# Four mixer groups streamed with a two-part moving operand, and a convolution's chain one slot sooner

## The chip, the core and the metric

The kernel runs on one core of a Trainium2 chip, in one launch. The metric is the time of an execution on the device in microseconds (us); the median of three runs stands below. The core's engines are TensorE (PE in the profile; its weight loads are PEld), VectorE (DVE), ScalarE (ACT), GpSimd (POOL) and SyncE (SP). Each runs its own list of instructions in order and waits on semaphores for the others.

## The reference, cut to what matters

256 positions of width 2048 go through one layer of a first block (four attention branches, gates, an output projection) and one layer of a second. The change lies in the second block's mixers, between the first block's output projection and the second's:

```
z = rms(h, norm_mix_g) @ w_in_2            # 2048 -> 4096 columns
za, zb, zc, zd = split(z, (1024, 2560, 3584))
# za: u, v = gelu(za);  oa = u * (tril(w_s) @ layernorm(v) + b_s)
# zb: h, bg, cg;        ob = bg * conv3(cg * h)
# zc: a, g;  h = conv31(a * sigmoid(g)) + b;  oc = silu(layernorm(h))
# zd: od = (windowed means of zd - zd) @ pool_w * pool_scale
h = h + concat(oa, ob, oc, od) @ w_out_2
```

Before it stand the attention branches, behind it a gated feed-forward of width 5632 and a last gated projection. Everything is float32 and nearly all of the time is matmuls.

## The kernel before, in words

**Units.** Each float32 matmul is made of three in the fp32r type: a weight W is split into a high part `hi` (a rounded copy by ACT, L855) and a low part `lo` = W - hi (DVE, L1244), the activations likewise into XH and XL (or YH and YL, MH and ML), and PE adds hi·XH, hi·XL and lo·XH. The weights come in 370 **units** of 128 x 2048 elements (1 MB), which `plan` (L66) lists in order. SP loads unit u into `raw[u % 5]` once unit u-5 is done, ACT makes `hi[u % 4]`, DVE makes `lo` (which takes raw's place), PE uses both. ACT and DVE work three units ahead (AHEAD): in step u each does its extra work of that step (`side(u)`), then splits unit u+3, then takes the finished group's result out of PSUM (`post`). PE does `side(u)`, then `unit(u)`.

**Kinds.** A group is a block of columns of a weight, in one of three kinds. "N" has the activations as the stationary operand. "T" has the weights stationary, and the result comes out transposed: 16 tiles of 128 x 128 in a unit, and for each three matmuls that stream 256 columns (`three`, L476 to L479), 48 in all. "T2", so far used for queries and keys alone, also has the weights stationary, but streams XH and XL as one operand of 512 columns (L530), so that hi·XH and hi·XL land beside each other in PSUM, and then, behind a wait for `lo`, lo·XH with 256 columns (L534): 16 and 16 matmuls in a unit. The two sums of a T2 group are added afterwards: ACT copies one out (L1091), DVE adds the other (L1653), one group being half as wide as a T group.

**PSUM.** Group results alternate between the two halves of `psA`; a group may start once the group two before it has been read (`bank_act`, `bank_dve`).

**The stretch of the change.** The groups after the first block's projection are cf 0 and 1 (units 170 to 177: the conformer's a and g, half each), v2 (178 to 181, kind N), u2 (182 to 185), zd (186 to 189), scc (190 to 193), sch (194 to 197), bg (198 to 201), then out2 (202 to 217). Beside them DVE works off the 31-tap convolution (`conv_tap`, L1443 and L1445): 124 instructions on 128 x 256, seven in a step from step 177 on, the last four in step 194. Their end lets PE sum over the channels (`channel_sum`, L749) in step 196. From there a chain goes back and forth: mean (ACT, L1045), centring (DVE, L1581), squares (ACT, L1047), second channel sum (PE, step 198), reciprocal root and scaling (DVE, step 198), affine and tanh (ACT, 199), product and parts (200). The pool mixer's sums stand in steps 194 and 195, its matmuls (L799) in 198. The parts of oa, ob, oc and od go to YH and YL, and out2 takes them in the order of MIX_ORDER.

Of the kernel before, what the change touches and what calls it, by code (L numbers as in the profile page):

```python
# [18 lines left out]
H = 4  # L19
# [43 lines left out]
MIX_ORDER = (0, 3, 2, 1)  # L63


def plan(A):  # L66
# [60 lines left out]
def build_hybrid(nc, A, C, out, scratch):  # L127
    with ExitStack() as ctx:
# [101 lines left out]
        SQ = PW[:, 0:2, :].rearrange("p g d -> p (g d)")  # L230
# [97 lines left out]
        def halves(g):  # L328

            name, n = g.name  # L330
            dst, n = (QI, n + 1) if name == "qi" else ({"q": QT, "k": KT}[name], n % 2)
            return dst[:, 2 * n:2 * n + 2, :]
# [10 lines left out]
        EARLY = (196, 199, 200)  # L343
# [131 lines left out]
        def tensor_program(e):  # L475
# [14 lines left out]
            def await_operand(g, i):  # L490
                name, n = g.name
                if name == "narrow" or g.kind == "T2":
                    e.wait_ge(xl_made, 2 * i + 2)
                elif name in ("qi", "z", "v", "q", "k", "gate"):
                    e.wait_ge(xl_made, i + 1)
                elif name == "branch":
                    e.wait_ge(flip_low, n % 4 + 1)
                elif name == "out":
                    e.wait_ge(flip_low, MERGED + i + 1)
                elif name in ("cf", "v2", "u2", "zd", "scc", "sch", "bg"):  # L500
                    e.wait_ge(flip_low, FIRST + i + 1)
                elif name == "out2":
                    e.wait_ge(mix_low, i + 1)
                elif name in ("fg", "fu"):
                    e.wait_ge(flip_low, SECOND + i + 1)
                elif name == "down":
                    e.wait_ge(flip_low, HIDDEN + 4 * (n // 4) + i + 1)
                elif name == "proj":
                    e.wait_ge(pt_made, 1)
                else:  # L510
                    e.wait_ge(flip_low, THIRD + i + 1)

            def unit(u):
# [12 lines left out]
                if g.kind == "T2":  # L526
# [6 lines left out]
                    for n, (c, kb, s, both) in enumerate(places):  # L533
                        x = e.matmul(both[:, 256:512], ll[:, s], XH[:, kb, :], start=False,  # L534
                                     stop=i == len(g.parts) - 1 and n >= 14, skip_group_check=True)
                    x.then_inc(unit_done, 1)
# [215 lines left out]
            def side(u):  # L752
# [87 lines left out]
        def scalar_program(e):  # L840
# [112 lines left out]
            def side(u):  # L953
# [58 lines left out]
                if u in (176, 185):  # L1012
                    h = (176, 185).index(u)
                    cs = slice(2 * h, 2 * h + 2)
                    e.wait_ge(bank_dve, freed(("cf", h)))
# [19 lines left out]
                if u == 191:  # L1035
                    e.wait_ge(bank_dve, freed(("u2", 0)))
                    gelu_inner(B[:, 3, :], B[:, 2, :])
# [5 lines left out]
                if u == 196:  # L1043
# [4 lines left out]
                if u == 198:  # L1048
                    e.wait_ge(pool_dotted, 1)
                    for g in range(4):  # L1050
                        x = e.activation(YH[:, 12 + g, :], c4(psB[:, 1, :])[:, g, :], ACT.Copy, scale=VC[:, 76 + g:77 + g])
                    x.then_inc(mix_high, 1)
                if u == 199:
# [5 lines left out]
                if u == 200:  # L1059
                    e.wait_ge(cn_made, 1)  # L1060
                    part_high(CA[:, :, :], 2, 0.5)
                if u in TURN2:
# [12 lines left out]
            def post(g):  # L1075
# [10 lines left out]
                elif g.kind == "T2":  # L1086
# [3 lines left out]
                    e.wait_ge(unit_done, g.last + 1)  # L1090
                    e.activation(halves(g), sums(g)[1], ACT.Copy).then_inc(crossed, 1)  # L1091
                elif name == "qi":
# [37 lines left out]
                elif name == "bg":  # L1130
                    e.wait_ge(bank_dve, g.freed)
                    part_high(c4(B[:, 3, :]), 1, 1.0)
# [68 lines left out]
        def vector_program(e):  # L1201
# [262 lines left out]
            def pool_sums():  # L1464
                e.memset(P1[:, :, 0:16], 0.0)
                e.memset(P2[:, :, 0:16], 0.0)
                e.wait_ge(bank_dve, freed(("zd", 0)))
# [15 lines left out]
            def side(u):  # L1483
# [90 lines left out]
                if u == 194:  # L1574
                    part_low(c4(B[:, 3, :]), 0, 0.5, 1)
                    pool_sums()
                if u == 195:
                    pool_means()
                if u == 196:
                    e.wait_ge(cm_made, 1)  # L1580
                    e.tensor_tensor(CA[:, :, :], CA[:, :, :], over(ST[:, 0, :], 4), ALU.subtract).then_inc(ca_centered, 1)  # L1581
                if u == 198:
# [4 lines left out]
                    e.tensor_tensor(CA[:, :, :], CA[:, :, :], over(y_, 4), ALU.mult).then_inc(ca_normed, 1)  # L1587
                    y = c4(B[:, 2, :])
# [6 lines left out]
                if u == 199:  # L1595
                    y = c4(B[:, 2, :])
                    for j in (1, 2):
                        for c in range(4):
# [3 lines left out]
                                                   op0=ALU.mult, op1=ALU.add).then_inc(short_taps, 1)  # L1602
                    e.wait_ge(short_taps, 12)
                    finish(e.tensor_tensor(y, y, over(SB[:, :], 4), ALU.mult))
                if u == 200:
                    e.wait_ge(cn_tanh, 1)
                    e.scalar_tensor_tensor(out=CA[:, :, :], in0=CB[:, :, :], scalar=1.0, in1=CA[:, :, :], op0=ALU.add,
                                           op1=ALU.mult).then_inc(cn_made, 1)
                    e.wait_ge(mix_high, 2)
# [4 lines left out]
                    part_low(CA[:, :, :], 2, 0.5, 3)  # L1614
# [28 lines left out]
            def post(g):  # L1643
# [6 lines left out]
                elif g.kind == "T2":  # L1650
                    dst = halves(g)
                    e.wait_ge(crossed, g.crossed)
                    x = e.tensor_tensor(dst, sums(g)[0], dst, ALU.add)  # L1653
                    if name == "k":
                        finish(x)
                        e.wait_ge(rx_copied, 1)
                        x = e.tensor_tensor(dst, dst, over(RX[:, :], 2), ALU.mult)
                    x.then_inc(bank_dve, 1)
                elif name == "branch":
# [19 lines left out]
                elif name == "cf":  # L1679
                    cs = slice(2 * n, 2 * n + 2)  # L1680
                    e.wait_ge(unit_done, g.last + 1)
                    e.wait_ge(sb_made, 1)
                    e.tensor_tensor(CA[:, cs, :], c4(ps)[:, 0:2, :], over(SB[:, :], 2), ALU.mult)
                    e.tensor_tensor(CB[:, cs, :], c4(ps)[:, 2:4, :], over(SB[:, :], 2), ALU.mult).then_inc(bank_dve, 1)
                elif name == "u2":
                    e.wait_ge(unit_done, g.last + 1)
                    e.tensor_tensor(c4(B[:, 3, :]), c4(ps), over(SB[:, :], 4), ALU.mult).then_inc(bank_dve, 1)
                elif name == "zd":
                    e.memset(PA[:, :, 0:16], 0.0)
                    e.wait_ge(unit_done, g.last + 1)  # L1690
                    e.tensor_tensor(PA[:, :, 16:272], c4(ps), over(SB[:, :], 4), ALU.mult).then_inc(bank_dve, 1)
# [13 lines left out]
                elif name == "bg":  # L1705
                    t = c4(B[:, 3, :])
                    e.wait_ge(unit_done, g.last + 1)
                    e.tensor_tensor(t, c4(ps), c4(B[:, 2, :]), ALU.mult).then_inc(bank_dve, 1)
                    part_low(t, 1, 1.0, 4)
# [148 lines left out]
```

## Time and profile before

| what | us |
|---|---|
| median of 3 runs (lowest, highest) | 2116.52 (2116.45, 2117.03) |
| the profiled execution, its own time | 2116.6 |
| its span, first to last instruction | 2114.8 |
| PE busy in the span | 2101.7 (99%), 10607 matmul records |
| DVE busy | 1215.1 (57%) |
| ACT busy | 901.8 (43%) |
| granted TensorE clock, mean | 0.999 of full |

The profile is of one execution. A page gives the busy time of each engine and the chain of work that ended last. The views of the trace used below give single instructions in order of time (the timeline), the busy time by stretch (windows), and that chain in order of time. A matmul's record lasts longer than the distance to the next one, since they overlap: the pace is read from starts. A float32 matmul that isn't fp32r shows as two records.

### The profile page before, as it was taken

How to read it: one execution, taken by the hardware profiler on the slowest of the kernel's cores; microseconds unless marked ns; L12 is line 12 of the kernel's file. 1: busy time of each engine (PE TensorE's matmuls, PEld its weight loads, DVE VectorE, ACT ScalarE, POOL GpSimd, SP SyncE). 2: the span in 40 equal slices, each digit the busy share in tenths (PEclk: the TensorE clock that was granted, in tenths of full speed). 3: DMA queues.
4: the chain of work that ended last, by engine and by line, in shares of the span. 5: the costliest groups of instructions: out<-in, count | busy, mean ns of one | idle time of the engine just before them, and what ended most of it. 6: DMA issues, size and time to landing. Idle time of an engine off the chain costs nothing.

```text
span 2114.8 us, 24862 instructions
## 1 busy us (share of the span) xinstructions
PE 2101.7 (99%) x10607; PEld 1788.5 (85%) x10607; DVE 1215.1 (57%) x1211; ACT 901.8 (43%) x858; POOL 21.1 (1%) x40
## 2 busy tenths in 40 slices
PE   9999999999999999999999999999999999999998
PEld 8888888888888888888999888888888888888887
DVE  5576555665545544456889855545445454454555
ACT  5444443544443443445354444343333433334443
POOL 2000000000000000000000000000000000000000
PEclk9999999999999999999999999999999999999999
DMA  8655555555655555575655556555555555565553
GB/s 245 212 178 178 166 171 182 171 175 173 199 182 196 192 188 197 192 246 180 206 187 171 179 179 195 189 187 191 198 188 191 184 194 196 187 195 182 195 201 120
DMA packets 224685, 398.34 MB, mean 188 GB/s; under 512 B 11154, under 2 KB 56458, under 8 KB 224320
## 3 DMA queue, kind: packets, MB, share of 16 engines
q1 hardware_dynamic: 221296, 387.64, 56.0%
q0 software_dynamic: 2528, 8.00, 1.3%
q8 instruction: 84, 1.38, 0.3%
q10 hardware_dynamic: 752, 1.12, 0.1%
q14 instruction: 25, 0.20, 0.0%
HBM read 394.62 MB, written 2.12 MB: 188 GB/s over the span
## 4 chain that ended last, share of the span: by engine, by line
PE 95%; DVE 4%; ACT 1%; issue 0%; ACTq 0%
PE psA L477 27%; PE psA L479 27%; PE psA L478 27%; PE psA L530 6%; PE psA L534 3%; DVE CA L1445 1%; PE psB L589 1%; DVE lo L1244 1%; PE psB L689 0%; PE psB L715 0%; PE psA L826 0%; PE psB L637 0%; PE psB L749 0%; ACT hi L855 0%; PE psB L676 0%
## 5 line engine op out<-in xcount | busy, mean ns | idle before, releaser
L1244 DVE TENSOR_TENSOR lo<-raw,hi 128x2048 fp32r<-128x2048 f32 x369 | 837.1, 2272 | 618.2 <-ACT hi L855 616.0
L855 ACT ACTIVATE hi<-raw 128x2048 fp32r<-128x2048 f32 x369 | 699.6, 1900 | 685.4 <-PE psA L479 583.2
L477 PE MATMUL psA<-hi,XHL 128*128 128x512 f32 x1632 | 637.9, 391 | 0.0
L479 PE MATMUL psA<-hi,XHL 128*128 128x512 f32 x1632 | 633.9, 388 | 0.0
L478 PE MATMUL psA<-lo,XHL 128*128 128x512 f32 x1632 | 633.4, 388 | 0.0
L479 PEld LDWEIGHTS psA<-hi,XHL 128*128 128x128 f32 x1632 | 306.3, 188 | 63.6
L477 PEld LDWEIGHTS psA<-hi,XHL 128*128 128x128 f32 x1632 | 306.5, 188 | 62.6 <-issue 0.4
L478 PEld LDWEIGHTS psA<-lo,XHL 128*128 128x128 f32 x1632 | 306.6, 188 | 61.7
L477 PE MATMUL psA<-hi,YH 128*128 128x512 f32 x608 | 237.2, 390 | 0.0
L479 PE MATMUL psA<-hi,YL 128*128 128x512 f32 x608 | 236.6, 389 | 0.0
L478 PE MATMUL psA<-lo,YH 128*128 128x512 f32 x608 | 236.6, 389 | 0.0
L477 PE MATMUL psA<-XHL,hi 128*128 128x256 f32 (+1 forms) x528 | 150.2, 284 | 1.2 <-DVE lo L1284 1.2
L478 PE MATMUL psA<-XHL,hi 128*128 128x256 f32 (+1 forms) x528 | 149.3, 283 | 0.0
L479 PE MATMUL psA<-XHL,lo 128*128 128x256 f32 (+1 forms) x528 | 149.3, 283 | 0.0
L530 PE MATMUL psA<-XHL,hi 128*128 128x512 f32 x576 | 138.6, 393 | 0.0
L479 PEld LDWEIGHTS psA<-hi,YL 128*128 128x128 f32 x608 | 114.1, 188 | 23.7
L477 PEld LDWEIGHTS psA<-hi,YH 128*128 128x128 f32 x608 | 114.1, 188 | 23.5
L478 PEld LDWEIGHTS psA<-lo,YH 128*128 128x128 f32 x608 | 114.2, 188 | 23.4
L530 PEld LDWEIGHTS psA<-XHL,hi 128*128 128x128 f32 x576 | 105.9, 188 | 21.5 <-issue 0.6
L477 PEld LDWEIGHTS psA<-XHL,hi 128*128 128x128 f32 (+1 forms) x528 | 100.7, 191 | 1.7 <-DVE XHL L1291 1.6
L478 PEld LDWEIGHTS psA<-XHL,hi 128*128 128x128 f32 (+1 forms) x528 | 100.7, 191 | 0.2
L479 PEld LDWEIGHTS psA<-XHL,lo 128*128 128x128 f32 (+1 forms) x528 | 100.7, 191 | 0.0
(355 smaller groups left out, 1273.6 us busy)
## 6 DMA issues: line engine op xcount, KB each, us to landing
raw<-in_w_in_dram SPq DMA_DIRECT2D x159, 1024.0 KB, 5.1
raw<-in_w_gate_dram SPq DMA_DIRECT2D x44, 1024.0 KB, 5.2
raw<-in_w_up_dram SPq DMA_DIRECT2D x44, 1024.0 KB, 5.2
raw<-in_w_down_dram SPq DMA_DIRECT2D x44, 1024.0 KB, 5.1
raw<-in_w_out_dram SPq DMA_DIRECT2D x32, 1024.0 KB, 5.1
raw<-in_w_branch_dram SPq DMA_DIRECT2D x16, 1024.0 KB, 5.0
raw<-in_w_ple_gate_dram SPq DMA_DIRECT2D x16, 1024.0 KB, 5.0
raw<-in_w_in_dram SPq DMA_DIRECT2D x16, 512.0 KB, 4.7
```

The lines of the kernel that those rows point to most:

```text
L477: e.matmul(dst, A2[0], B2[0], start=first, stop=False, skip_group_check=True)
L478: e.matmul(dst, A2[0], B2[1], start=False, stop=False, skip_group_check=True)
L479: return e.matmul(dst, A2[1], B2[0], start=False, stop=last, skip_group_check=True)
L530: e.matmul(both, hh[:, s], XHL[:, kb, :, :].rearrange("p a t -> p (a t)"), start=i == 0 and n < 2, stop=False, skip_group_check=True)
L534: x = e.matmul(both[:, 256:512], ll[:, s], XH[:, kb, :], start=False, stop=i == len(g.parts) - 1 and n >= 14, skip_group_check=True)
L589: x = e.transpose(ps[:, k, 128 * t:128 * t + 128], src(t, k), ID[:, :])
L855: e.activation(hi[u % H][:, 0:m], raw[u % R][:, 0:m], ACT.Copy).then_inc(hi_made, 1)
L1244: e.tensor_tensor(lo[u % R][:, 0:m], raw[u % R][:, 0:m], hi[u % H][:, 0:m].bitcast(F32), ALU.subtract).then_inc(lo_made, 1)
L1445: x = e.scalar_tensor_tensor(out=CA[:, c, :], in0=HP[:, c, j:j + 256], scalar=CW[:, 4 * j + c:4 * j + c + 1], in1=CA[:, c, :], op0=ALU.mul ...
```

## The change

- In `plan`, cf 1 becomes two T2 groups (cf 1: the a half, cf 2: the g half, both of the second 256 columns), and u2, zd and bg become two T2 groups each. They cover the same units as before (174 to 177, 182 to 189, 198 to 201); a unit is now 8 blocks of rows by 256 columns instead of 4 by 512. The count of groups grows by four.
- The T groups that stay (cf 0, scc, sch) do all hi·XH and hi·XL of a unit first, then wait for `lo`, then do the 16 lo·XH.
- The first channel sum of PE moves from step 196 to 195, the second from 198 to 197, and the steps of ACT and DVE that hang on them with them (centring before the pool's means; scaling in 197; affine and tanh in 198; product in 199). The 124 taps stay in the steps where they were.
- The pool's first sums move from step 194 to 195 and its means from 195 to 196; its matmuls stay in 198. out2 takes the blocks in the order 0, 2, 3, 1.
- `post` of the new T2 groups: an ACT copy, a DVE addition and a DVE product (with SB, or for bg with the short convolution) for each half.

```diff
-MIX_ORDER = (0, 3, 2, 1)
+MIX_ORDER = (0, 2, 3, 1)
@@ plan
-    for h in range(2):
-        group(("cf", h), "T", w_in2, (2560 + 256 * h, 3072 + 256 * h), K16)
+    group(("cf", 0), "T", w_in2, (2560, 3072), K16)
+    for n in (1, 2):
+        group(("cf", n), "T2", w_in2, 2304 + 512 * n, K8)
...
-        group((name, 0), "T", w_in2, col, K16)
+        if name in ("scc", "sch"):
+            group((name, 0), "T", w_in2, col, K16)
+        else:
+            for h in range(2):
+                group((name, h), "T2", w_in2, col + 256 * h, K8)
@@ tensor_program, unit
-                if g.kind == "T2":
+                if g.kind == "T2" or g.kind == "T" and u >= H:
                     e.wait_ge(hi_made, u + 1)
...
+                if g.kind == "T" and u >= H:
...
+                    for j, c, kb, s, dst in places:
+                        e.matmul(dst, hh[:, s], XH[:, kb, :], start=i == 0 and j == 0 and c % 2 == 0, stop=False,
+                                 skip_group_check=True)
+                        e.matmul(dst, hh[:, s], XL[:, kb, :], start=False, stop=False, skip_group_check=True)
+                    e.wait_ge(lo_made, u + 1)
+                    for j, c, kb, s, dst in places:
+                        x = e.matmul(dst, ll[:, s], XH[:, kb, :], start=False, stop=i == len(g.parts) - 1 and j == 3,
+                                     skip_group_check=True)
...
@@ tensor_program, side
-                if u == 196:
+                if u == 195:
                     e.wait_ge(conv_taps, 124)
                     e.wait_ge(sw_made, 1)
                     channel_sum(psB[:, 0, 0:256], CA, cm_dotted)
...
-                if u == 198:
+                if u == 197:
                     e.wait_ge(cv_squared, 1)
                     channel_sum(psB[:, 0, 512:768], CB, var_dotted)
@@ vector_program, side
                 if u == 194:
                     part_low(c4(B[:, 3, :]), 0, 0.5, 1)
+                if u == 195:
                     pool_sums()
-                if u == 195:
-                    pool_means()
-                if u == 196:
                     e.wait_ge(cm_made, 1)
                     e.tensor_tensor(CA[:, :, :], CA[:, :, :], over(ST[:, 0, :], 4), ALU.subtract).then_inc(ca_centered, 1)
-                if u == 198:
+                if u == 196:
+                    pool_means()
+                if u == 197:
@@ vector_program, post
                 elif g.kind == "T2":
                     dst = halves(g)
+                    if name == "zd" and n == 0:
+                        e.memset(PA[:, :, 0:16], 0.0)
                     e.wait_ge(crossed, g.crossed)
                     x = e.tensor_tensor(dst, sums(g)[0], dst, ALU.add)
...
+                    elif name in ("cf", "u2", "zd"):
+                        finish(x)
+                        e.wait_ge(sb_made, 1)
+                        x = e.tensor_tensor(dst, dst, over(SB[:, :], 2), ALU.mult)
                     x.then_inc(bank_dve, 1)
...
-                    e.tensor_tensor(c4(B[:, 3, :]), c4(ps), over(SB[:, :], 4), ALU.mult).then_inc(bank_dve, 1)
```

The order on PE around the first channel sum, before. L477, L478 and L479 are hi·XH, lo·XH and hi·XL (the operands' printed order is moving, then stationary), L744 the sgu mixer's eight matmuls behind unit 193, L749 the channel sum; between L744 and L749 stand units 194 and 195, 96 matmuls:

```order
L744 MATMUL psB<-SW,B 128x128 x8
L477 MATMUL psA<-XHL,hi 128x256
L478 MATMUL psA<-XHL,hi 128x256
...
L479 MATMUL psA<-XHL,lo 128x256
L749 MATMUL psB<-CA,TR 128x256 x4
L477 MATMUL psA<-XHL,hi 128x256
```

And after (L554 and L556 are hi·XH and hi·XL, L559 lo·XH, L769 the mixer's matmuls, L774 the channel sum):

```order
L769 MATMUL psB<-SW,B 128x128 x8
L554 MATMUL psA<-XHL,hi 128x256
L556 MATMUL psA<-XHL,hi 128x256
...
L559 MATMUL psA<-XHL,lo 128x256 x16
L774 MATMUL psB<-CA,TR 128x256 x4
L554 MATMUL psA<-XHL,hi 128x256
```

The channel sum now has one unit (194) between it and the mixer's matmuls, where it had two.

The order on DVE from u2's result to zd's, before (L1687 reads u2 out of PSUM, L1691 zd; SM rows of a small reciprocal root left out):

```order
L1687 TENSOR_TENSOR B<-psA,SB 128x1024
L1443 TENSOR_SCALAR CA<-HP,CW,VC 128x256 x2
L1445 SCALAR_TENSOR_TENSOR CA<-HP,CW,CA 128x256 x7
...
L1244 TENSOR_TENSOR lo<-raw,hi 128x2048
L1689 MEMSET B 128x4x16
L1691 TENSOR_TENSOR B<-psA,SB 128x4x256
```

After (L1682 adds a half's two sums, L1693 multiplies by SB, L1270 makes `lo`, L1469 and L1471 are the taps). First u2's second half, then zd's first and second:

```order
L1682 TENSOR_TENSOR B<-psA,B 128x512
L1693 TENSOR_TENSOR B<-B,SB 128x512
L1469 TENSOR_SCALAR CA<-HP,CW,VC 128x256 x2
L1471 SCALAR_TENSOR_TENSOR CA<-HP,CW,CA 128x256 x7
...
L1682 TENSOR_TENSOR B<-psA,B 128x2x256
L1693 TENSOR_TENSOR B<-B,SB 128x2x256
...
L1270 TENSOR_TENSOR lo<-raw,hi 128x2048
L1682 TENSOR_TENSOR B<-psA,B 128x2x256
L1693 TENSOR_TENSOR B<-B,SB 128x2x256
```

One instruction of 128 x 1024 has become four of 128 x 512, two for each half, and the first half's pair stands two splits ahead of the second's; u2's first pair stands in step 183.

## Rows read from the trace of the kernel before

**Rows 1.** The page: busy time; the chain that ended last, by engine.

```profile
PE 2101.7 (99%) x10607; PEld 1788.5 (85%) x10607; DVE 1215.1 (57%) x1211; ACT 901.8 (43%) x858; POOL 21.1 (1%) x40
...
PE 95%; DVE 4%; ACT 1%; issue 0%; ACTq 0%
```

**Rows 2.** Windows: length; busy PE, PEld, DVE, ACT, POOL; the second, DVE alone.

```profile
1107.00:1153.00 46.00, 45.75 (x376) 45.34 (x376) 45.62 (x71) 18.55 (x13) 0.00 (x0) 1.00 0.52 163
...
1087.10:1143.60 56.50, 55.95 (x96) 1.00 0.55 179
```

**Rows 3.** PE's timeline: first matmuls of units 190, 191, 195; channel sum.

```profile
1106.95 0.28 PE L477 MATMUL psA<-XHL,hi 128*128 128x256 f32 x1
...
1112.71 0.28 PE L477 MATMUL psA<-XHL,hi 128*128 128x256 f32 x1
...
1137.53 0.28 PE L477 MATMUL psA<-XHL,hi 128*128 128x256 f32 x1
...
1143.70 1.99 PE L749 MATMUL psB<-CA,TR 128*128 128x256 f32 x8 [0.25 <-DVE CA L1445]
```

**Rows 4.** PE's timeline: T2 units 51 and 52, hi part.

```profile
318.48 3.82 PE L530 MATMUL psA<-XHL,hi 128*128 128x512 f32 x16
...
324.04 3.82 PE L530 MATMUL psA<-XHL,hi 128*128 128x512 f32 x16
```

**Rows 5.** DVE's timeline, 1065 to 1144: waits, posts, taps.

```profile
1065.27 2.29 DVE L1244 TENSOR_TENSOR lo<-raw,hi 128x2048 fp32r<-128x2048 f32 x1 [2.02 <-ACT hi L855]
...
1087.07 2.29 DVE L1244 TENSOR_TENSOR lo<-raw,hi 128x2048 fp32r<-128x2048 f32 x1 [3.52 <-ACT hi L855]
1089.28 1.22 DVE L1687 TENSOR_TENSOR B<-psA,SB 128x1024 f32<-128x1024 f32 x1
1090.41 0.73 DVE L1443 TENSOR_SCALAR CA<-HP,CW,VC 128x256 f32<-128x256 f32 x2
...
1103.73 2.86 DVE L1445 SCALAR_TENSOR_TENSOR CA<-HP,CW,CA 128x256 f32<-128x256 f32 x7
...
1113.73 0.11 DVE L1689 MEMSET B<- 128x64 f32 x1
...
1114.83 2.86 DVE L1445 SCALAR_TENSOR_TENSOR CA<-HP,CW,CA 128x256 f32<-128x256 f32 x7
...
1141.98 1.67 DVE L1445 SCALAR_TENSOR_TENSOR CA<-HP,CW,CA 128x256 f32<-128x256 f32 x4
```

**Rows 6.** DVE's timeline: a key half's post; a product of 128 x 512.

```profile
347.20 0.69 DVE L1653 TENSOR_TENSOR KT<-psA,KT 128x512 f32<-128x512 f32 x1 [1.96 <-ACT KT L1091]
347.93 0.69 DVE L1657 TENSOR_TENSOR KT<-KT,RX 128x512 f32<-128x512 f32 x1
...
1039.90 0.68 DVE L1684 TENSOR_TENSOR CB<-psA,SB 128x512 f32<-128x512 f32 x1
1040.50 2.85 DVE L1445 SCALAR_TENSOR_TENSOR CA<-HP,CW,CA 128x256 f32<-128x256 f32 x7
```

**Rows 7.** ACT's timeline, ahead of DVE's two waits.

```profile
1061.08 0.69 ACT L1125 ACTIVATE B<-psA,SM 128x512 f32<-128x512 f32 x1 [3.23 <-PE psA L479]
...
1063.34 1.90 ACT L855 ACTIVATE hi<-raw 128x2048 fp32r<-128x2048 f32 x1
...
1083.58 0.40 ACT L1026 ACTIVATE B<-B,SM 128x128 f32<-128x128 f32 x1 [8.47 <-DVE SM L1560]
```

**Rows 8.** Windows at the end; the granted clock is third from last.

```profile
2105.00:2106.00 1.00, 0.20 (x2) 0.00 (x0) 0.20 (x1) 0.77 (x3) 0.00 (x0) 1.00 1.02 379
...
2109.00:2110.00 1.00, 0.00 (x0) 0.00 (x0) 0.93 (x3) 0.64 (x2) 0.00 (x0) 0.73 0.00 0
2110.00:2112.00 2.00, 0.00 (x0) 0.00 (x0) 0.51 (x2) 0.70 (x2) 0.00 (x0) 0.50 0.52 194
```

**Rows 9.** PE's timeline at the start: the same float32 matmul first and later.

```profile
2.02 4.64 PE L826 MATMUL psA<-QI 128*128 128x256 f32 x10 [2.02 <-DVE QI L1751]
...
8.61 1.89 PE L831 MATMUL psB<-QI 128*128 128x256 f32 x8
```

More of the change, by code:

```diff
@@ L330, in halves @@
             name, n = g.name
-            dst, n = (QI, n + 1) if name == "qi" else ({"q": QT, "k": KT}[name], n % 2)
+            if name == "cf":
+                return (CA, CB)[n - 1][:, 2:4, :]
+            if name == "zd":
+                return PA[:, 2 * n:2 * n + 2, 16:272]
+            n = n + 1 if name == "qi" else n % 2
+            dst = {"qi": QI, "q": QT, "k": KT}[name] if name in ("qi", "q", "k") else c4(B[:, 3, :])
             return dst[:, 2 * n:2 * n + 2, :]
@@ L491, in await_operand @@
                 name, n = g.name
-                if name == "narrow" or g.kind == "T2":
+                if name in ("narrow", "qi", "q", "k") and len(g.parts) == 2:
                     e.wait_ge(xl_made, 2 * i + 2)
+                elif g.kind == "T2":
+                    e.wait_ge(flip_low, FIRST + 2 * i + 2)
                 elif name in ("qi", "z", "v", "q", "k", "gate"):
@@ L535, in unit @@
                                      stop=i == len(g.parts) - 1 and n >= 14, skip_group_check=True)
+                    x.then_inc(unit_done, 1)
+                    return
+                if g.kind == "T" and u >= H:
+                    places = [(j, c, kb, slice(512 * j + 128 * c, 512 * j + 128 * c + 128), ps[:, 256 * c:256 * c + 256])
+                              for j, (_, kb) in enumerate(part) for c in range(4)]
+                    for j, c, kb, s, dst in places:
[6 more added lines that the diff above has]
+                                     skip_group_check=True)
                     x.then_inc(unit_done, 1)
@@ L1048, in side @@
                 if u == 198:
[L1049 to L1053, printed above, removed]
                     e.wait_ge(ca_normed, 1)
@@ L1058, in side @@
                     e.activation(CB[:, :, :], CA[:, :, :], ACT.Tanh, scale=0.5).then_inc(cn_tanh, 1)
-                if u == 200:
+                if u == 199:
                     e.wait_ge(cn_made, 1)
                     part_high(CA[:, :, :], 2, 0.5)
+                    e.wait_ge(pool_dotted, 1)
+                    for g in range(4):
+                        x = e.activation(YH[:, 12 + g, :], c4(psB[:, 1, :])[:, g, :], ACT.Copy, scale=VC[:, 76 + g:77 + g])
+                    x.then_inc(mix_high, 1)
                 if u in TURN2:
@@ L1090, in post @@
                     e.wait_ge(unit_done, g.last + 1)
+                    if name == "bg":
+                        e.wait_ge(pool_dotted, 1)
                     e.activation(halves(g), sums(g)[1], ACT.Copy).then_inc(crossed, 1)
+                    if name == "bg" and n == 1:
+                        e.wait_ge(bank_dve, g.freed)
+                        part_high(c4(B[:, 3, :]), 1, 1.0)
                 elif name == "qi":
@@ L1587, in side @@
                     e.tensor_tensor(CA[:, :, :], CA[:, :, :], over(y_, 4), ALU.mult).then_inc(ca_normed, 1)
+                if u == 198:
                     y = c4(B[:, 2, :])
@@ L1595, in side @@
                 if u == 199:
+                    e.wait_ge(cn_tanh, 1)
+                    e.scalar_tensor_tensor(out=CA[:, :, :], in0=CB[:, :, :], scalar=1.0, in1=CA[:, :, :], op0=ALU.add,
+                                           op1=ALU.mult).then_inc(cn_made, 1)
                     y = c4(B[:, 2, :])
@@ L1605, in side @@
                 if u == 200:
[L1606 to L1609, printed above, removed]
+                    e.wait_ge(mix_high, 3)
                     for g in range(4):
@@ L1679, in post @@
                 elif name == "cf":
-                    cs = slice(2 * n, 2 * n + 2)
                     e.wait_ge(unit_done, g.last + 1)
                     e.wait_ge(sb_made, 1)
[L1683 to L1686, printed above, removed]
-                    e.tensor_tensor(c4(B[:, 3, :]), c4(ps), over(SB[:, :], 4), ALU.mult).then_inc(bank_dve, 1)
[L1688 to L1691, printed above, removed]
+                    e.tensor_tensor(CA[:, 0:2, :], c4(ps)[:, 0:2, :], over(SB[:, :], 2), ALU.mult)
+                    e.tensor_tensor(CB[:, 0:2, :], c4(ps)[:, 2:4, :], over(SB[:, :], 2), ALU.mult).then_inc(bank_dve, 1)
                 elif name == "scc":
```

27 lines of the change are left out of this document (12 added, 15 removed).

## The prediction

> **What bounds the kernel now.** First the page: PE is busy for 2101.7 of 2114.8 us and the chain that ended last lies on PE for 95% [rows 1]. So in general only PE's pace counts. Then the windows of the stretch that is changed: from 1107 to 1153 us PE is busy 45.75 of 46.00 us, but DVE 45.62 of 46.00 [rows 2]. Here two engines are full at once, and the 4% of the chain on DVE come from such places. Then PE's timeline around the channel sum: it starts at 1143.70 after 0.25 us of idleness that a DVE write of CA ended, the last tap of the convolution [rows 3], which ended at 1141.98 + 1.67 = 1143.65 [rows 5]. So in the kernel before the taps are just in time for step 196, with nothing to spare. DVE itself has no gap from 1087.07 to there: 55.95 busy of 56.50 us [rows 2], the rest being the short pauses between dependent instructions.
>
> **What T2 gives PE.** A T unit takes 1112.71 - 1106.95 = 5.76 us from start to start [rows 3], a T2 unit 324.04 - 318.48 = 5.56 [rows 4]. Sixteen units change kind (4 of cf, 4 of u2, 4 of zd, 4 of bg): 16 x 0.20 = 3.2 us, all on PE's path where PE is never short of operands. These rows say that per tile 512 columns at once cost 12 ns less than twice 256.
>
> The Trainium skill, page TensorE: Matmul & The Clock Gate, section Back-to-back issue gap, gives an isolated matmul N / 2.4 ns + 2.5 ns, by which a merged pair would save only 2.5 ns in a tile, about 0.04 us in a unit and 0.6 us in all where the rows give 3.2; the rows disagree with it, and the sum goes by the rows.
>
> **What `lo` last gives.** In the 12 T units that stay, the wait for `lo` comes two thirds of a unit later. No wait for `lo` shows on PE in the stretch before; same matmuls, same pace: nothing. Four groups more mean no more units or matmuls. The loads have other shapes, but each is issued five units, some 28 us, ahead, and of that `hi` and `lo` take 1.90 and 2.29 [rows 5, 7]: nothing. The order of out2's blocks follows the order in which they get ready: nothing.
>
> **What it costs DVE.** A product of 128 x 1024 out of PSUM takes 1.13 us of DVE for u2 (1089.28 to 1090.41) and 1.10 with its memset for zd (1113.73 to 1114.83) [rows 5]. A T2 half takes an addition (0.73 from its start to that of the next, dependent instruction) and a product (0.60, from 1039.90 to 1040.50) [rows 6], 1.33 in all. Four halves are 5.3 instead of 2.2: 3.1 us more before the last tap. Bounds: the product is 0.60 back to back and 0.73 with a pause, so 3.1 to 3.6. cf's halves (2.7 for 1.2) lie mostly in DVE's gaps before 1065, covered by its wait of 2.02 us there [rows 5]; bg's come after the taps.
>
> What gives DVE time back: that wait of 2.02 us at 1065.27 was ended by ACT's `hi` of 1063.34, which stood behind ACT's copies of v2 from 1061.08, released by PE [rows 5, 7]. PE gets there 4 units x 0.20 = 0.8 us sooner. The second wait (3.52 us, at 1087.07) was DVE's own doing: ACT's squares waited 8.47 us for a DVE result of gelu's chain, and `hi` stood behind them [rows 5, 7]; this round moves with DVE and stays as long. So the last tap moves by 3.1 - 0.8 = +2.3 us, to 1145.95.
>
> **What moving the channel sum costs PE.** This is the term that decides. The sum is now wanted one unit sooner, but the taps keep their steps and end 2.3 us later. From the start of the sum on PE has left what it had, and unit 195 too (5.76), less 4 bg units x 0.20 = 0.8. The end therefore moves by 2.3 + 5.76 - 0.8 = +7.3 us. Seen from PE: unit 194 ended at 1137.53 [rows 3]; with 12 T2 units before it, 2.4 us sooner, 1135.1. One small wait comes in between: unit 190 needs the half of PSUM that zd's first half used, and DVE reads it late: the taps at 1103.73 are preceded by it, so 1103.73 - 0.8 + 2 x 1.33 (u2's halves) - 1.13 + 0.05 + 0.73 + 0.69 = 1105.9, where PE arrives at 1106.95 - 2.4 = 1104.5: 1.4 us [rows 3, 5, 6]. PE then stands before the sum at 1136.5 and waits until 1145.95: 9.5 us, in place of 0.25. The wait at 190 isn't added, since it shortens the wait at 195.
>
> Queued behind the waiting sum is everything on PE: units 195 and on. ACT and DVE go on splitting ahead and fill their slots, so nothing else is late when PE starts again; the later steps of the chain keep their two-unit distance (195 to 197, where before 196 to 198) with the same matmuls. Step 198's pool matmuls get their operands in step 196, with two units to spare. I count these at 0; at worst one of them waits up to 3 us.
>
> **The clock.** PE's last matmul ends at 2105.2; the granted clock is still full until 2109 and at 0.50, that is 1.2 instead of 2.4 GHz, from within 2109 to 2110 on [rows 8]. A wait of 9.5 us is over twice that, so PE will find itself at half clock when the taps are done. No wait in the middle of the kernel before is long enough to show the way back. The start shows it: the first ten records of a 256-column float32 matmul took 4.64 us, eight of the same later 1.89, so ten would have been 2.3 [rows 9]: 2.3 us lost before the pace is full. I add 2.3, with 0 (the clock holds) and about 3.5 (the low level lasts half as long again) as ends.
>
> The Trainium skill says the same thing as a warning, in TensorE: Matmul & The Clock Gate, section Why this matters for your kernels: idle gaps between bursts of matmuls drop the array back to the lower clock. By this rule the sum is 9.6 us, without it 7.3; the trace agrees with it at the end of the kernel.
>
> **The sum.** Against the profiled execution: its span 2114.8 + 7.3 + 2.3 = 2124.4, and 1.8 around the span as before: 2126.2. Its time of 2116.6 is the median within 0.1, so the forecast is 2126.1 us, 9.6 (0.45%) more than 2116.52.
>
> **The rivals.**
> 1. The clock holds, or recovers at once: 2116.5 + 7.3 = 2123.8. For it: the mechanism is seen only at the ends of the kernel. Against it: the fall came 4 us into idleness there, and 9.5 are due here. 12%.
> 2. Not slower: DVE gets through in time and the sum doesn't wait. Then only 3.2 + 0.25 remain: 2116.5 - 3.4 = 2113.1, which is within 0.2%. This decides at the last tap: it would have to end by 1136.5 instead of 1145.95. Speaking for it would be slack in DVE's list, and the windows show 0.5 us of pauses in 56 [rows 2]; each tap depends on the one before the last on the same columns. 4%. That the change doesn't do what it says belongs here with its other sign: were the two-part operand no faster than two matmuls, as the skill's formula has it, DVE would get 0.2 back instead of 0.8 and bg save 0.2 instead of 0.8, which gives 2126.1 + 1.2 = 2127.3. 2%.
> 3. A second wait opens behind the first (centring behind the pool's sums, the second channel sum, or the pool's matmuls), up to 3 us: 2129. For it: DVE is still full until 1153 [rows 2]. Against it: PE's stop of 9.5 us lets DVE and ACT get ahead. 8%.
>
> **How the numbers follow.** Forecast 2126.1: 71%, own range 2124.8 to 2127.8 from the bounds of the clock and of the halves. Rivals 12, 4, 2, 8; the rest, 3%, is spread. The range 2122.5 to 2128.5 holds the forecast, the first rival and the skill's formula. A measurement of this kernel can tell about 0.2%, 4.2 us, from no change; the first rival and the third lie beyond it on the same side. Slower 0.93, same 0.06, faster 0.01.
>
> **What would show it.** Before the first channel sum PE idles 9 to 10 us, ended by a tap; before unit 190 1.4 us, ended by DVE's product of zd's first half; the granted clock falls to 0.50 in that wait and PE's matmuls run at half pace for some 4.6 us behind it; T2 units start 5.56 us apart; DVE is without gaps from 1088 to the last tap. I am wrong if the last tap ends before 1140, or if the wait before the sum is under 5 us; wrong in one term if the matmuls behind it keep their full pace.

## The result, and the profile after

| | median us (lowest, highest) |
|---|---|
| before, run beside it | 2116.48 (2116.40, 2117.03) |
| after | 2125.89 (2125.58, 2126.18) |
| ratio | 1.0043, 95% interval 1.0031 to 1.0056 |

The changed kernel is 9.4 us (0.43%) slower, and the interval of the ratio lies clear of 1. The profiled execution took 2125.58 us, with a span of 2123.8. Beside the experiments below the kernel before had medians of 2116.61 to 2116.75.

The page first: busy time of each engine, and the engines of the chain that ended last.

```profile
PE 2100.5 (99%) x10351; PEld 1776.7 (84%) x10351; DVE 1221.1 (57%) x1222; ACT 906.6 (43%) x866; POOL 21.2 (1%) x40
...
PE 95%; DVE 4%; ACT 1%; issue 0%; ACTq 0%
```

Against [rows 1] PE has 256 records fewer (16 units in which 32 matmuls became 16) and is busy 1.2 us less, while the span grew by 9.0. The shares are the same as before. A page on which PE is busy for 99% does not show where 9 us went; the waits of PE from 1040 to 1215 us do (line waited at, who ended it, total, times, longest):

```profile
PE psB L774 <- DVE CA L1471: 9.1, 1, 9.1
PE psA L554 <- DVE B L1693: 1.3, 1, 1.3
```

Two waits, and nothing else. In PE's timeline around them, first two T2 units of zd, then the first unit behind the short wait (190) and the next, then the end of unit 194, the channel sum behind the long wait, and the first matmuls of unit 195 behind it:

```profile
1093.31 3.82 PE L542 MATMUL psA<-XHL,hi 128*128 128x512 f32 x16
...
1098.88 1.32 PE L542 MATMUL psA<-XHL,hi 128*128 128x512 f32 x5
...
1105.90 0.35 PE L554 MATMUL psA<-XHL,hi 128*128 128x256 f32 x1 [1.30 <-DVE B L1693]
...
1111.73 0.28 PE L554 MATMUL psA<-XHL,hi 128*128 128x256 f32 x1
...
1134.63 2.08 PE L559 MATMUL psA<-XHL,lo 128*128 128x256 f32 x16
...
1145.82 3.78 PE L774 MATMUL psB<-CA,TR 128*128 128x256 f32 x8 [9.11 <-DVE CA L1471]
...
1149.04 0.74 PE L554 MATMUL psA<-XHL,hi 128*128 128x256 f32 x1
1149.61 0.28 PE L556 MATMUL psA<-XHL,hi 128*128 128x256 f32 x1
```

The T2 units start 5.57 us apart. The sum starts at 1145.82, where in the kernel before it started at 1143.70 with a whole unit more in front of it [rows 3]. From its start to the next unit's it takes 3.22 us, before 1.65 (1143.70 to 1145.35).

Windows of the same stretch (length; busy PE, PEld, DVE, ACT, POOL; granted clock; DMA share, GB/s):

```profile
1107.00:1153.00 46.00, 36.89 (x287) 35.97 (x287) 45.59 (x66) 17.90 (x15) 0.00 (x0) 0.89 0.42 132
...
1138.00:1139.00 1.00, 0.00 (x0) 0.00 (x0) 1.00 (x2) 0.00 (x0) 0.00 (x0) 1.00 0.79 152
1139.00:1140.00 1.00, 0.00 (x0) 0.00 (x0) 1.00 (x1) 0.00 (x0) 0.00 (x0) 0.68 0.92 310
...
1140.00:1145.00 5.00, 0.00 (x0) 0.00 (x0) 4.93 (x8) 0.79 (x1) 0.00 (x0) 0.50 0.31 110
1145.00:1149.00 4.00, 3.18 (x8) 2.56 (x9) 3.80 (x4) 3.87 (x3) 0.00 (x0) 0.50 0.00 0
1149.00:1150.00 1.00, 1.00 (x7) 0.91 (x6) 1.00 (x4) 0.36 (x1) 0.00 (x0) 0.70 0.00 0
1150.00:1151.00 1.00, 1.00 (x11) 1.00 (x10) 0.97 (x2) 0.02 (x1) 0.00 (x0) 1.00 0.00 0
```

Against [rows 2] PE is busy 36.89 of 46 us in place of 45.75, DVE as full as before. The granted clock falls to 0.50 (1.2 GHz) within 1139 to 1140, while PE stands, and is back at 1.00 (2.4 GHz) within 1149 to 1150, after some 3.8 us of matmuls. By the shares of these two windows it fell at about 1139.4, 2.7 us after PE's last record ended (1134.63 + 2.08 = 1136.71).

And DVE's timeline: the first wait of [rows 5], u2's two halves (1072.66, 1089.68), zd's two (1104.40, 1115.62), and the last taps.

```profile
1064.34 2.29 DVE L1270 TENSOR_TENSOR lo<-raw,hi 128x2048 fp32r<-128x2048 f32 x1 [1.26 <-ACT hi L880]
...
1072.66 0.68 DVE L1682 TENSOR_TENSOR B<-psA,B 128x512 f32<-128x512 f32 x1
1073.37 0.69 DVE L1693 TENSOR_TENSOR B<-B,SB 128x512 f32<-128x512 f32 x1
...
1087.47 2.29 DVE L1270 TENSOR_TENSOR lo<-raw,hi 128x2048 fp32r<-128x2048 f32 x1 [3.52 <-ACT hi L880]
1089.68 0.68 DVE L1682 TENSOR_TENSOR B<-psA,B 128x512 f32<-128x512 f32 x1
1090.40 0.69 DVE L1693 TENSOR_TENSOR B<-B,SB 128x512 f32<-128x512 f32 x1
...
1104.40 0.63 DVE L1682 TENSOR_TENSOR B<-psA,B 128x512 f32<-128x512 f32 x1
1105.07 0.69 DVE L1693 TENSOR_TENSOR B<-B,SB 128x512 f32<-128x512 f32 x1
...
1115.62 0.69 DVE L1682 TENSOR_TENSOR B<-psA,B 128x512 f32<-128x512 f32 x1
1116.35 0.69 DVE L1693 TENSOR_TENSOR B<-B,SB 128x512 f32<-128x512 f32 x1
...
1144.10 1.67 DVE L1471 SCALAR_TENSOR_TENSOR CA<-HP,CW,CA 128x256 f32<-128x256 f32 x4
```

The second wait of 3.52 us is as long as before [rows 5] and 0.40 later. The last tap ends at 1144.10 + 1.67 = 1145.77, 2.12 later than before, and DVE has no gap from 1087.47 to there.

### The profile page after: what moved, and what is told of

It reads as the page before. It is cut to its first block, busy times and chain, and to the rows that moved or that the text cites. A ratio compares the mean times of both kernels' runs of the same rounds, so it can differ in the third digit from the quotient of the medians.

```text
span 2123.8 us, 24372 instructions
## 1 busy us (share of the span) xinstructions
PE 2100.5 (99%) x10351; PEld 1776.7 (84%) x10351; DVE 1221.1 (57%) x1222; ACT 906.6 (43%) x866; POOL 21.2 (1%) x40
## 3 DMA queue, kind: packets, MB, share of 16 engines
HBM read 394.62 MB, written 2.12 MB: 187 GB/s over the span
## 4 chain that ended last, share of the span: by engine, by line
PE 95%; DVE 4%; ACT 1%; issue 0%; ACTq 0%
PE psA L487 26%; PE psA L489 26%; PE psA L488 26%; PE psA L542 8%; PE psA L546 4%; DVE CA L1471 1%; PE psB L614 1%; DVE lo L1270 1%; PE psA L554 1%; PE psA L559 1%; PE psA L556 1%; PE psB L774 0%; PE psB L714 0%; PE psB L740 0%; PE psA L851 0%
## 5 line engine op out<-in xcount | busy, mean ns | idle before, releaser
L1270 DVE TENSOR_TENSOR lo<-raw,hi 128x2048 fp32r<-128x2048 f32 x369 | 837.2, 2272 | 618.2 <-ACT hi L880 616.0
L542 PE MATMUL psA<-XHL,hi 128*128 128x512 f32 x832 | 200.0, 392 | 0.0
L542 PEld LDWEIGHTS psA<-XHL,hi 128*128 128x128 f32 x832 | 153.1, 188 | 30.8 <-issue 0.6
L546 PEld LDWEIGHTS psA<-XHL,lo 128*128 128x128 f32 x832 | 106.7, 191 | 4.1
L546 PE MATMUL psA<-XHL,lo 128*128 128x256 f32 x832 | 107.9, 283 | 0.0
L487 PE MATMUL psA<-hi,MH 128*128 128x512 f32 x128 | 50.2, 392 | 0.0
L489 PE MATMUL psA<-hi,ML 128*128 128x512 f32 x128 | 49.9, 390 | 0.0
L488 PE MATMUL psA<-lo,MH 128*128 128x512 f32 x128 | 49.8, 389 | 0.0
L1471 DVE SCALAR_TENSOR_TENSOR CA<-HP,CW,CA 128x256 f32<-128x256 f32 x120 | 49.0, 479 | 0.0
```

The costliest lines, as they stand in the source:

```text
L487: e.matmul(dst, A2[0], B2[0], start=first, stop=False, skip_group_check=True)
L488: e.matmul(dst, A2[0], B2[1], start=False, stop=False, skip_group_check=True)
L489: return e.matmul(dst, A2[1], B2[0], start=False, stop=last, skip_group_check=True)
L542: e.matmul(both, hh[:, s], XHL[:, kb, :, :].rearrange("p a t -> p (a t)"), start=i == 0 and n < 2, stop=False, skip_group_check=True)
L1270: e.tensor_tensor(lo[u % R][:, 0:m], raw[u % R][:, 0:m], hi[u % H][:, 0:m].bitcast(F32), ALU.subtract).then_inc(lo_made, 1)
L1471: x = e.scalar_tensor_tensor(out=CA[:, c, :], in0=HP[:, c, j:j + 256], scalar=CW[:, 4 * j + c:4 * j + c + 1], in1=CA[:, c, :], op0=ALU.mul ...
```

## The experiments

**The theory:** the 9.4 us are the sum wanted a unit sooner (5.76), the taps 2.3 us later, the clock that falls in the wait (about 2), less what bg gains (0.8). **The rivals:** the clock costs nothing; DVE's additional halves alone bring the loss; `lo` last costs or gives something; the merged operand gives nothing.

### The change with the chain in its old steps

```diff
-                if u == 195:
+                if u == 196:
                     e.wait_ge(conv_taps, 124)
...
-                if u == 197:
+                if u == 198:
                     e.wait_ge(cv_squared, 1)
```

and the steps of ACT and DVE that hang on them, the pool's steps and MIX_ORDER as before the change. The rest is the changed kernel.

> The changed kernel with the convolution's chain put back into the steps it had before (sums in steps 196 and 198, and what hangs on them); the T2 groups and lo last stay. Last-tap theory: the taps still end near 1145.7 on DVE (2.1 us later than before), PE reaches the sum one unit later, near 1142.4, and waits some 3.4 us; the end is 2.1 - 0.8 (four bg units at 0.2) = 1.3 us behind the kernel before: 2117.8 us; the wait is shorter than the 4 us after which the clock fell at the kernel's end, so the clock should hold. Rival, the T2 groups themselves are slow (their reading out of PSUM, their loads): the time stays near 2125.9.

Measured: 2119.84 us (2118.69 to 2120.82), ratio 1.0014 (1.0005 to 1.0023). The profiled execution is the 2118.69 one. PE's timeline at the sum:

```profile
1146.53 1.99 PE L774 MATMUL psB<-CA,TR 128*128 128x256 f32 x8 [3.35 <-DVE CA L1472]
```

And windows around it, columns as above:

```profile
1143.00:1146.00 3.00, 0.17 (x2) 0.00 (x0) 2.96 (x7) 1.08 (x2) 0.00 (x0) 1.00 0.49 115
1146.00:1148.00 2.00, 1.47 (x7) 1.32 (x8) 2.00 (x6) 2.00 (x2) 0.00 (x0) 1.00 0.98 339
```

In this execution the clock holds through the wait of 3.35 us. It starts 0.7 us late, in its first matmuls (16 transposes take 2.51 us where they took 1.97 in the kernel after); without that it stands at 2118.0, close to the 2117.8 that the terms gave. But the other nine executions are 1.0 to 2.1 us above the profiled one, with a mean clock of 0.998 or 0.997 instead of 0.999. I take it from this that the clock fell in them; none of the nine has a profile, so it is inferred and not shown. The chain's step is worth about 6 us (2125.89 - 2119.84), most of the loss. The median lies 2.0 us above what I expected, and by this reading the clock after a wait of 3.4 us is what I had wrong.

### The chain alone

The kernel before with the chain's edit alone (the diff above the other way round); all groups T.

> The kernel before with the convolution's chain one step sooner and nothing else. Last-tap theory: the taps end at 1143.65 as before, PE is there at 1137.5 and waits some 6 us; unit 195 comes behind the sum: + 5.8 us, and the clock, if 6 us of idleness are enough for it to fall, + 2.0: 2124.2 (2122.2 if it holds). Rival, the T2 groups are what is slow: 2116.5.

Measured: 2124.91 us (2123.95 to 2125.08), ratio 1.0037 (1.0024 to 1.0051). PE's timeline:

```profile
1143.70 3.57 PE L749 MATMUL psB<-CA,TR 128*128 128x256 f32 x8 [6.01 <-DVE CA L1444]
```

The taps end where they ended before [rows 5], the wait is a unit's 5.76 us + 0.25, and the sum takes 3.57 instead of 1.99: half clock. One edit alone makes 8.3 of the 9.4 us (2124.91 - 2116.61). In the profiled execution it is 7.3 us of span, the unit's 5.76 and 1.6 of half clock. The other four executions are 0.7 to 1.1 us slower than the profiled one, and no profile shows why; the expected 2124.2 was 0.7 short of the median.

### Matmuls in the wait, to keep the clock up

The changed kernel with 18 float32 matmuls of 256 columns ahead of the wait. They write where the sum writes afterwards, so their results are dropped.

```diff
                 if u == 195:
+                    e.wait_ge(sw_made, 1)
+                    for _ in range(18):
+                        e.matmul(psB[:, 0, 0:256], ONE, SB[:, :], start=True, stop=True)
                     e.wait_ge(conv_taps, 124)
```

> The changed kernel with 18 matmuls of 128x256 in float32 on PE ahead of the wait for the last tap, whose result the channel sum overwrites: about 7.8 us of work in a wait of 9.1. If the half clock behind the wait costs 2 us of its own, the clock now stays full, PE waits about 1.3 us, the sum's eight records take 2 us instead of 3.8, and the time is 2123.9. If the half clock is harmless, the time stays 2125.9; if the added matmuls don't fit into the wait, it is more.

Measured: 2124.24 us (2123.73 to 2124.52), ratio 1.0035 (1.0021 to 1.0048). PE's timeline:

```profile
1137.01 7.93 PE L817 MATMUL psB<-SB,TR 128*128 128x256 f32 x36
...
1146.30 1.99 PE L774 MATMUL psB<-CA,TR 128*128 128x256 f32 x8 [1.35 <-DVE CA L1474]
```

And two windows:

```profile
1136.00:1145.00 9.00, 8.95 (x46) 7.66 (x45) 8.93 (x14) 1.88 (x3) 0.00 (x0) 1.00 0.40 117
1145.00:1151.00 6.00, 4.70 (x33) 4.50 (x34) 5.80 (x9) 4.62 (x4) 0.00 (x0) 1.00 0.00 0
```

The taps end when they end, so the sum starts no sooner (it stands 0.5 us later than in the kernel after, since this execution was 0.5 us later from its first matmuls on). But it takes 1.99 us instead of 3.78, and the kernel is 1.65 us faster with 36 more matmul records. That difference of medians is what the half clock cost.

### Taps taken away

The changed kernel without 28 of the 124 taps, four in each of steps 187 to 193, so its result isn't the reference's.

```diff
-                    e.wait_ge(conv_taps, 124)
+                    e.wait_ge(conv_taps, 96)
...
-                    for j, c in some:
+                    for j, c in (some[:3] if 187 <= u <= 193 else some):
```

> The changed kernel without 28 of the 124 taps (four in each of steps 187 to 193), so the convolution's result is not the reference's; 28 x 0.395 = 11 us of DVE work less ahead of the last tap. Last-tap theory: the wait of 9.1 us is gone and with it the half clock, and what is left is the gain of 16 T2 units and the 0.25 us: 2113.0 to 2114 us, faster than the kernel before. Rival, something else in the moved chain or the new groups costs time: it stays above 2116.5.

Measured: 2113.22 us (2112.77 to 2113.64), ratio 0.9983 (0.9974 to 0.9993). PE waits nowhere from 1040 to 1215 us, and the sum follows unit 194 at once:

```profile
1133.12 2.08 PE L559 MATMUL psA<-XHL,lo 128*128 128x256 f32 x16
1135.05 1.89 PE L774 MATMUL psB<-CA,TR 128*128 128x256 f32 x8
```

Everything else of the change is in this kernel. So nothing of its loss lies in the loads, in `lo` last, in the order of the blocks or in a later step of the chain: it is that DVE ends the taps late.

### `lo` last alone

The kernel before; the 28 T units of its mixers do hi·XH and hi·XL first, then wait for `lo` (the branch of the change's diff). In the kernel before, L477, L478 and L479 are hi·XH, hi·XL and lo·XH, in this order: the third operand pair of each tile is what moves to the end. (The section on the change has L478 and L479 the wrong way round.)

> The kernel before with the other order inside its T units alone (hi parts first, then the wait for lo, then the 16 lo matmuls; 28 units of cf, u2, zd, scc, sch, bg), still 48 matmuls of 256 columns in a unit. My theory: no wait for lo showed on PE, same pace, 2116.5 as before within 0.3 us. Rival: the order brings something by itself (the same stationary tile twice in a row happens in both orders' hi part only now), then a T unit takes less than 5.76 us from start to start and the time falls by up to 3 us.

Measured: 2116.80 us (2116.27 to 2117.17), ratio 1.0000 (0.9990 to 1.0009). Beside it the kernel before had 2116.75. Nothing is gained and nothing lost that these runs can tell.

### T2 where DVE has time

The chain as before, `lo` last, T2 for cf 1 and bg alone; u2 and zd stay T with one product each, read out as before the change. The line in `plan`, against the first experiment's kernel:

```diff
-        if name in ("scc", "sch"):
+        if name in ("scc", "sch", "u2", "zd"):
```

> Two-part streaming for cf 1 and bg alone, u2 and zd as they were, the chain in the steps of before, lo last in the T units. Theory that the end is set by DVE up to the last tap: u2's and zd's halves are what made the taps later (3.1 us); without them the taps end 0.8 us sooner than before (1142.9), and bg's gain of 0.8 comes on top: 2116.5 - 1.6 = 2114.9, with a wait of 0.2 us before the sum. Rival, PE's pace sets it everywhere: 8 units less of T2 than in the first experiment make it slower than that one (2119.8), by 1.6 us: 2121.4.

Measured: 2115.15 us (2114.81 to 2115.68), ratio 0.9993 (0.9983 to 1.0002). PE waits for 0.27 us before the sum, as in the kernel before; the last taps start at 1141.11 instead of 1141.98. Eight units at 0.20 give 1.6 us (2116.75 - 2115.15), and they are kept, since their halves lie in DVE's gaps or behind the taps.

### Nine taps into DVE's own wait

To the change with the chain in its old steps comes a move on DVE: the second block's wait of 3.52 us is for ACT's squares, which stand behind DVE's means in step 185. The nine taps of step 186 (the first step of each half of the convolution has nine, the last four, those between seven) are put between, in step 185.

```diff
-                if u in CONV:
+                if u in CONV and u != 186:
...
                     e.tensor_scalar(gm, gm, -1.0 / 128, None, ALU.mult).then_inc(sgu_mean, 1)
+                    for j, c in CONV[186][1]:
+                        conv_tap(2 + c, j)
```

> The first experiment (all T2 groups, lo last, the chain in the steps of before), and the nine taps of step 186 put into step 185, into DVE's wait of 3.5 us for hi behind the mean of the sgu mixer. They take 3.4 us, so the last tap ends near 1142.3 to 1143 instead of 1146.5, and the wait of PE before unit 190 is gone too. Expected: PE waits some 1 to 2 us before the sum, too short for the clock to fall: 2114.5 to 2115. If DVE's wait was not idle time that taps can use (ACT's hi comes later then), the time stays at 2118.7 to 2119.8.

Measured: 2115.31 us (2114.74 to 2116.73), ratio 0.9995 (0.9986 to 1.0004). Six executions lie at 2114.74 to 2115.36, four at 2116.65 to 2116.73, so the median is one of a mixture; it lies above the expected 2114.5 to 2115. The profiled one is one of the four. PE's timeline at the sum:

```profile
1142.95 3.14 PE L774 MATMUL psB<-CA,TR 128*128 128x256 f32 x8 [1.78 <-DVE CA L1472]
```

And windows behind it:

```profile
1142.00:1143.00 1.00, 0.05 (x1) 0.05 (x1) 1.00 (x4) 1.00 (x2) 0.00 (x0) 1.00 0.62 122
1143.00:1144.00 1.00, 1.00 (x4) 0.88 (x5) 1.00 (x2) 1.00 (x1) 0.00 (x0) 0.82 0.89 230
...
1144.00:1147.00 3.00, 3.00 (x11) 2.55 (x11) 2.93 (x6) 3.00 (x3) 0.00 (x0) 0.50 0.68 232
1147.00:1148.00 1.00, 1.00 (x10) 1.00 (x10) 1.00 (x1) 1.00 (x2) 0.00 (x0) 0.97 0.00 0
```

Here the wait is 1.78 us, and the clock falls all the same, in 1143 to 1144, when PE is at work again. In this execution a wait of 1.78 us did not protect the clock. PE's wait before unit 190 is gone, as expected.

### And the first taps one step sooner

On top of that the first half's taps start in step 176 instead of 177, and each of its later steps takes the taps that follow:

```diff
-        CONV = {177 + 9 * h + i: (h, TAPS[2 + CHUNK * i if i else 0:2 + CHUNK * i + CHUNK]) for h in range(2) for i in range(9)}
+        SOON = ((9, 16, 23, 30, 37, 44, 51, 58, 62, 62), (0, 9, 16, 23, 30, 37, 44, 51, 58, 62))
+        CONV = {177 + 9 * h + i: (h, TAPS[SOON[h][i]:SOON[h][i + 1]]) for h in range(2) for i in range(9)}
...
                     conv_start(0)
+                    for j, c in TAPS[0:9]:
+                        conv_tap(c, j)
```

> The same, and the first nine taps of the convolution's first half moved from step 177 to 176, where DVE waited for hi before; every later step of that half does the taps of the step behind it, and step 185 none of them. No arithmetic is left out. 3.4 us less of DVE work in its full stretch; the last tap ends before PE gets to the sum in step 196, so PE should wait nowhere in the stretch and keep the whole gain of the 16 T2 units and the 0.25 us: 2113.0 to 2113.5, faster than both kernels. If another chain becomes the bound, a new wait shows on PE and the time lies above 2114.

Measured: 2112.89 us (2112.80 to 2113.43), ratio 0.9982 (0.9973 to 0.9992). This kernel is faster than both. The timeline, PE's sum and DVE's last taps:

```profile
1141.13 1.89 PE L775 MATMUL psB<-CA,TR 128*128 128x256 f32 x8
...
1138.74 1.67 DVE L1473 SCALAR_TENSOR_TENSOR CA<-HP,CW,CA 128x256 f32<-128x256 f32 x4
```

And the window that answers to [rows 2]:

```profile
1107.00:1153.00 46.00, 46.00 (x380) 45.79 (x380) 45.59 (x68) 15.85 (x13) 0.00 (x0) 1.00 0.56 176
```

The taps end at 1140.41, 0.7 us before they are wanted. PE is busy for the whole 46 us.

### Which part of that is the taps' own

The two moves of taps in the kernel before, all groups T:

> The kernel before with the two moves of taps of e10 alone (nine taps from step 176 on, nine in DVE's wait of step 185); all groups T, chain in its old steps. Theory: the kernel before loses 0.25 us at the channel sum and nothing else in this stretch, so taps that are done sooner can give back 0.25 us at most: 2116.2 to 2116.6. The gain of e10 is then the 3.2 us of the T2 units, which the taps only uncover. Rival: the order of the taps is worth something by itself (shorter waits of PE elsewhere); then this kernel is at 2114.5 or lower and e10 has only part of its gain from T2.

Measured: 2116.07 us (2115.86 to 2116.15), ratio 0.9997 (0.9987 to 1.0006). PE's timeline:

```profile
1143.22 1.89 PE L750 MATMUL psB<-CA,TR 128*128 128x256 f32 x8
```

The taps end at 1137.42, nearly 6 us too early, and it gives 0.6 us. Unit starts of the two traces differ by a steady 0.07 us up to unit 195, and by 0.58 from 196 on: the wait of 0.25 us cost twice its length, which I had not allowed for, and so the time is 0.1 us below the end of my range. The moves are worth 0.6 us by themselves; the other 3.2 us that separate this kernel from the last (2116.07 - 2112.89) are T2's, since `lo` last gives nothing.

And the same moves in the changed kernel, with its chain one step sooner:

> The changed kernel, chain one step sooner included, with the same two moves of taps. Theory: the taps end where they ended in e10, near 1140.4, but PE is before the sum one unit sooner, near 1135, and waits about 5.3 us, against e10's none; with the clock falling in that wait (about 2 us) the time is 2112.9 + 5.3 + 2 = 2120.2, or 2118.2 in executions in which the clock holds. Rival: with the taps sooner the chain's sooner step costs nothing any more, or pays: 2112.9 or lower.

Measured: 2120.43 us (2119.73 to 2120.93), ratio 1.0017 (1.0007 to 1.0026). PE's timeline:

```profile
1140.28 3.63 PE L775 MATMUL psB<-CA,TR 128*128 128x256 f32 x8 [4.90 <-DVE CA L1472]
```

The taps end where they ended in the kernel with the old steps, within 0.2 us, and the sooner step costs 7.5 us (2120.43 - 2112.89). In the two profiled executions the spans differ by 6.6 (2118.0 and 2111.4): 5.1 of waiting by starts and 1.7 of half clock, less 0.2 by which this execution was ahead from the start. The rest of the 7.5 lies between executions, and no profile shows it. Where the taps are in time for it, in the kernel with 28 fewer, it gives nothing either (2113.22 against 2112.89). In these two kernels PE waits for nothing behind the sum, so there an earlier step has nothing to gain.

## Why the prediction came true, step by step

The forecast was 2126.1, the result 2125.89; the steps held one by one. Their sizes, in the profiled execution:

| step | forecast | measured |
|---|---|---|
| T2 unit, start to start | 5.56 | 5.57 (1093.31 to 1098.88) |
| twelve T2 units before the taps' end | -2.4 | -2.3 (start of unit 190 in the last kernel above) |
| wait before unit 190 | 1.4 | 1.30 in the view, 1.45 from starts |
| last tap ends | 1145.95 | 1145.77 |
| wait before the sum | 9.5 | 9.11 in the view, 9.3 from starts |
| half clock | +2.3 | +1.85 |
| `lo` last | 0 | 0 (2116.80 against 2116.61 to 2116.75) |
| later waits | 0 | none in the waits of PE |

**The last tap** came out to the tenth, counted from equal starts: this execution of after runs 0.18 us ahead of that of before until unit 174, so 2.12 is 2.30 from equal starts. DVE's first wait shrank (2.02 to 1.26) and what stood behind it came 0.9 us sooner; the four halves took 0.67 to 0.73 for the addition and 0.60 or 0.61 for the product, from start to start.

**The wait.** Unit 194's last 16 matmuls start at 1134.63 and take 1.92 from start to start, so the sum could have started at 1136.55; it started 9.27 later. The view says 9.11 because it counts from the end of the last matmul's record, which lies 0.16 behind the next possible start (a record of 0.28 us, a distance of 0.12). For a stop of PE the starts are the better measure: the 0.25 us of [rows 3] put the sum off by 0.41 (1143.70 against 1137.53 + 5.76), and what followed by 0.5.

**The clock** is the one term mis-sized. Two units after the sum PE is at these rows, the first of before, the second of after:

```profile
1157.04 1.89 PE L799 MATMUL psB<-B,PW 128*128 128x256 f32 x8
...
1161.01 1.89 PE L774 MATMUL psB<-CB,TR 128*128 128x256 f32 x8
```

From the sum's start it took 13.34 us before (1143.70 to 1157.04) and 15.19 after (1145.82 to 1161.01), 1.85 more. Of that 1.57 lie in the sum (3.22 against 1.65), the rest in the unit behind it. The beginning of the kernel [rows 9] had said 2.3, and half pace for 4.6 us where it lasted 3.8. The runs with matmuls in the wait put the difference of medians at 1.65.

**What is luck in the last digits.** With the measured sizes the terms give 2.30 + 5.76 - 0.8 + 1.85 = 9.1 us, and the profiled executions show 9.2 (spans 9.0 apart, and that of after began 0.2 ahead). The medians are 9.4 apart, since the other executions of the changed kernel are slower than the profiled one by 0.1 to 0.6 us, which no profile explains. That the forecast of 9.6 came within 0.2 of them owes something to a clock term that was 0.45 too large.

**Rival 1** (the clock holds) had its price nearly right: 2123.8 was forecast, 2124.24 is the run in which the clock was made to hold. It didn't come true: the clock fell within 1139 to 1140, with 6 us of the wait still to come.

**Rival 2** (DVE on time) was priced at 2113.1; with the taps on time it is 2113.22 in one kernel and 2112.89 in the other. Its second form, that one operand of 512 columns is no faster than two of 256, is refuted by the T2 units' 5.57 us from start to start and by the 3.2 us that remain beside the taps' own gain. The Trainium skill (TensorE: Matmul & The Clock Gate, Back-to-back issue gap) says of its formula itself that it holds for isolated matmuls, and that with weight loads between them the spacing is set by both. The starts in this trace agree that the formula isn't the spacing here: they lie 228 and 120 ns apart for 512 and 256 columns, 11 to 12 more than an estimate by the formula (216 and 109). That it is the weight load that makes this difference no run here shows.

**Rival 3** (a second wait) did not appear.

**What was not foreseen** is on the other side of the forecast: the steps taken alone. I had taken a wait of 3.4 us as too short for the clock to fall, since at the kernel's end it fell 4 us into idleness. By the times it fell in nine executions of ten, and in four of ten with a wait of 1.8 us, one of which a profile shows. The one reading at the kernel's end was no measure: in the kernel after the clock fell 2.7 us after PE's last record, in the chain alone 2.4 us (its granted clock is 0.55 from 1140 to 1141, and PE's last record ended at 1137.69). The Trainium skill (TensorE: Matmul & The Clock Gate, section Why this matters for your kernels) warns of idle gaps between bursts of matmuls. The trace with the wait of 1.78 us agrees with it for a shorter gap than I had reckoned with; the one with 3.35 us, in which the clock held, shows that not every such gap brings a fall.

## What to carry to other kernels

Before a consumer is put in an earlier slot, look when its last producer ends: here PE already waited 0.25 us for it, and a slot of 5.76 us sooner could only become a wait. Ask also who waits for the consumer's result; where nobody did, as here, the earlier slot gained nothing even with the taps in time. And a gain on the bounding engine that is paid with work on another must be paid where that other has gaps: the same T2 units were worth 3.2 us as soon as taps had been moved forward into DVE's own waits.

## What the runs showed of the hardware

- The granted clock fell from 2.4 to 1.2 GHz in the profiled executions with a stop of PE of 9.11, 6.01, 4.90 and 1.78 us, and held in those with 3.35 and 1.35. In those not profiled the times speak for a fall in nine of ten with 3.4 us and in four of ten with 1.8. With 1.78 us it fell some 0.7 us after PE had gone back to work. PE was at work again for 3 to 4 us before the clock was back.
- A fall cost 1.6 to 1.9 us in the four profiles that show one, after 1.78 us of waiting as after 9.11.
- A stop that the view gives as 0.25 us cost 0.5 us in starts.
- At full clock a matmul of 512 columns with its weight load follows the last in 228 ns (3.65 us for 16, 1093.31 to 1096.96), one of 256 columns in 120 ns (1.92 for 16). Twice 256 is 12 ns more, 0.19 us in a unit of 16: this is the whole gain of T2.
